# One stage for four of the five projections of the second block, 44 weight tiles through two slots, on one Trainium2 core

## The chip, the core and the metric

The kernel runs on one core of one Trainium2 chip. The metric is the device time of one execution in microseconds (us), the median of several executions of the same program. Below, PE is the matrix engine (TensorE), PEld its weight loads, ACT the scalar engine, DVE the vector engine, POOL the GpSimd engine and SP the engine that issues most of the DMAs (SPq is its queue).

## The reference

Two blocks run one after the other on x [1, 2048, 1024], all in float32. The first is a gated delta rule in both directions beside windowed attention. The change lies in the second, of which this is the part that matters:

```python
IN_SIZES = (D_ATT, D_ATT, D_ATT, D_ATT, D_CONV, D_CONV, D_CONV, D_CONV, D_MODEL, D_MODEL)  # 8 x 512, 2 x 1024
...
h = rmsnorm(x, norm_g[l])
proj = jnp.einsum('bsd,de->bse', h, w_in[l])                    # [2048, 1024] x [1024, 6144]
q, k, v, z_att, gb, gc, u, z_conv, g_att, g_conv = jnp.split(proj, IN_SPLITS, axis=-1)
att = chunked_rel_attention(q, k, v, rel_bias[l])
y_att = jnp.einsum('bsc,cd->bsd', att * jax.nn.silu(z_att), w_att_out[l])
vconv = causal_depthwise_conv(gc * u, conv_w[l], conv_b[l])     # 3 taps along the sequence
y_conv = jnp.einsum('bsc,cd->bsd', gb * vconv * jax.nn.silu(z_conv), w_conv_out[l])
m = jax.nn.sigmoid(g_att) * y_att + jax.nn.sigmoid(g_conv) * y_conv
x = x + jnp.einsum('bsd,de->bse', m, w_out[l])
```

## The kernel before

The program is a row of stages. Each stage is a `Ctx` (line 68): it takes its SBUF, PSUM and semaphores, runs a block with one instruction stream for each engine, waits for its last stores, and ends by clearing its semaphores and with a barrier over all engines (`__exit__`, line 78; the branches of line 79 in the rows stand for it). Nothing of a stage runs before the barrier of the one before it.

The stage group `dense2` in `build` (from line 2612) computes h and its products with `w_in_2`:

- `norm_transpose` ("n2", tiles named n_ in the profile) writes h transposed, as a rounded part `hi` and a remainder `lo`, [128, 8, 2048] each. Both stay in SBUF for the whole group.
- `project_features` "pq": queries and keys, 8 weight tiles, copied out.
- `project_rows` "pv": values, with the tokens on the partitions.
- `project_features` "pz": the gate z_att, 4 weight tiles, silu.
- `project_gated_conv` "gc": gc, u, gb and z_conv, 16 weight tiles, four for each of four groups of 128 channels.
- `project_features` "ps": the sigmoid gates, 16 weight tiles.

Chunk attention ("ca") follows. A weight tile is 1024 inputs by 128 outputs, [128, 8, 128], 512 KB. SP loads it into one of two slots (`wraw0`, `wraw1`), ACT rounds it (`whi`, lines 2100 and 2186), DVE makes the remainder (`wlo`, lines 2121 and 2214), and PE computes `feature_tile`: 4 column groups x 8 k x 3 products (hi*hi, hi*lo, lo*hi, lines 106 to 108) = 96 matmuls of 512 columns into a PSUM tile `pp0` or `pp1` of [128, 2048], four banks. The two slots alternate, so while PE works on one, the other is evicted and gets its next weights:

```python
for s in S:
    act.wait_ge(product[s], j + 1 + START)
    if more:
        split_hi(j + 1, s)
    act.wait_ge(stored[s], 16 * j + START)
    nc.scalar.activation(ob[s][:], pp[s][:], func).then_inc(copied[s], 1)
```

SP's queue in such a stage is, for each pair of tiles, two loads (each after the remainder of the tile before it in that slot exists) and then two stores (each after its eviction). In "gc" the order of a group is: gc is copied by ACT (line 2192), DVE multiplies it by u from PSUM (2227), runs three taps (2231, 2236), multiplies by gb from PSUM (2240) and, once ACT has made silu of z_conv (2202), by that (2246); SP then stores `acc` (2175). ACT, DVE and SP go through the first N - 1 steps in a hardware loop, PE through all of them, with 192 matmuls in a pass of its loop (384 in "gc"). `project_rows` (line 363) has its own loads, four pieces of 512 KB (line 399).

Of the kernel before, what the change touches and what calls it, by code (L numbers as in the profile page):

```python
# [30 lines left out]
ALU = mybir.AluOpType  # L31
# [3 lines left out]
P = 128  # L35
# [2097 lines left out]
def project_gated_conv(nc, w_tiles, conv_w, hi, lo, out):  # L2133

    PAD = 2
    with Ctx(nc, "gc") as c:
        raw, whi, wlo = weight_tiles(c)
        S = range(2)
        cw = c.sb("cw", [P, 4, 4])
        gcb = c.sb("gcb", [P, SEQ])  # L2140
        gu = c.sb("gu", [P, SEQ + PAD])
        acc = c.sb("acc", [P, SEQ])
        sz = c.sb("sz", [P, SEQ])
# [10 lines left out]
        gb_done = c.sem("gb_done")  # L2154
        z_done = c.sem("z_done")
        y_done = c.sem("y_done")
        stored = c.sem("stored")
        block = c.stack.enter_context(nc.Block())
        N = 4

        @block.sync
        def _(sp):
            sp.dma_start(cw[:], conv_w).then_inc(cw_in, 16)
            for s in S:
                sp.dma_start(raw[s][:], w_tiles[s]).then_inc(w_in[s], 16)

            def step(i, more):
                for q in range(4):
                    s = q % 2
                    if more or q < 2:  # L2170
                        sp.wait_ge(lo_ready[s], 2 * i + q // 2 + 1 + START)
                        sp.wait_ge(cw_in, 16 + START)
                        sp.dma_start(raw[s][:], w_tiles[4 * i + (2 + q)]).then_inc(w_in[s], 16)
                sp.wait_ge(y_done, i + 1 + START)
                sp.dma_start(out[i], acc[:]).then_inc(stored, 16)

            with sp.Fori(0, N - 1) as i:
                step(i, True)
            step(N - 1, False)
            sp.wait_ge(stored, 16 * N + START)  # L2180

        @block.scalar
        def _(act):
            def split_hi(n, s):
                act.wait_ge(w_in[s], 16 * n + 16 + START)
                nc.scalar.copy(whi[s][:], raw[s][:]).then_inc(hi_ready[s], 1)

            def step(i, more):
                act.wait_ge(product[0], 2 * i + 1 + START)
                split_hi(2 * i + 1, 0)  # L2190
                act.wait_ge(gu_done, i + START)
                nc.scalar.copy(gcb[:], pp[0][:]).then_inc(gc_copied, 1)
                act.wait_ge(product[1], 2 * i + 1 + START)
                split_hi(2 * i + 1, 1)
                act.wait_ge(product[0], 2 * i + 2 + START)
                if more:
                    split_hi(2 * i + 2, 0)
# [551 lines left out]
```

## Time and profile before

| what | value |
|---|---|
| median of 3 runs | 3802.14 us (3794.01 to 3803.87) |
| the profiled execution | 3789.2 us, span 3787.1 us |
| mean granted clock of PE | 0.923 of full |
| PE busy | 3256.6 us, 86% of the span |
| PE weight loads busy | 2696.8 us, 71% |
| DVE busy | 1307.0 us, 35% |
| ACT busy | 1081.6 us, 29% |
| POOL busy | 339.1 us, 9% |
| DMA | 382.43 MB, mean 101 GB/s |

The span is what the profiler saw of one execution; the device time of that execution is 2.1 us more, for what lies around it. Times within it are counted from the start of the span. The busy shares are means over stages with different limits, so the stretch from 1969 us (the first matmul of "pq") to 3101 us (the first of chunk attention) has to be read by itself. The ends of matmuls are modelled: a matmul of 512 columns is shown as 0.39 us while the next one starts earlier.

### The profile page before, as it was taken

How to read it: one execution, taken by the hardware profiler on the slowest of the kernel's cores; microseconds unless marked ns; L12 is line 12 of the kernel's file. 1: busy time of each engine (PE TensorE's matmuls, PEld its weight loads, DVE VectorE, ACT ScalarE, POOL GpSimd, SP SyncE). 2: the span in 40 equal slices, each digit the busy share in tenths (PEclk: the TensorE clock that was granted, in tenths of full speed). 3: DMA queues.
4: the chain of work that ended last, by engine and by line, in shares of the span. 5: the costliest groups of instructions: out<-in, count | busy, mean ns of one | idle time of the engine just before them, and what ended most of it. 6: DMA issues, size and time to landing. Idle time of an engine off the chain costs nothing. (4 is left out here: it accounts for less than half of the span.)

```text
span 3787.1 us, 60889 instructions
## 1 busy us (share of the span) xinstructions
PE 3256.6 (86%) x24054; PEld 2696.8 (71%) x24054; DVE 1307.0 (35%) x2392; ACT 1081.6 (29%) x2146; POOL 339.1 (9%) x316
## 2 busy tenths in 40 slices
PE   6996889754999973978959888999899979969899
PEld 5775779754999971546848777888688856747677
DVE  5554000263555547665540000111100015553343
ACT  4222111232444433871131111001022127740032
POOL 0000000001233224013200000000000001120000
PEclk8998999886999995998979999999999979989999
DMA  3122111384333334315531111010012133044453
GB/s 106 67 67 80 64 61 60 115 288 152 103 137 120 123 102 128 113 62 168 181 128 67 72 61 67 30 37 33 33 67 78 66 121 94 14 150 156 171 172 122
DMA packets 218819, 382.43 MB, mean 101 GB/s; under 512 B 34976, under 2 KB 143264, under 8 KB 202528
## 3 DMA queue, kind: packets, MB, share of 16 engines
q1 hardware_dynamic: 176512, 343.94, 26.6%
q10 hardware_dynamic: 42144, 36.18, 3.0%
q8 instruction: 119, 1.95, 0.2%
q14 instruction: 44, 0.36, 0.0%
HBM read 237.98 MB, written 142.08 MB: 100 GB/s over the span
## 5 line engine op out<-in xcount | busy, mean ns | idle before, releaser
L106 PE MATMUL ps_pp<-h_hi,ps_whi 128*128 128x512 f32 x512 | 200.1, 391 | 15.2 <-DVE ps_wlo L2121 15.2
L106 PE MATMUL gc_pp<-h_hi,gc_whi 128*128 128x512 f32 x512 | 200.2, 391 | 13.4 <-DVE gc_wlo L2214 13.4
L107 PE MATMUL ps_pp<-h_lo,ps_whi 128*128 128x512 f32 x512 | 199.9, 390 | 0.0
L107 PE MATMUL gc_pp<-h_lo,gc_whi 128*128 128x512 f32 x512 | 199.9, 390 | 0.0
L108 PE MATMUL gc_pp<-h_hi,gc_wlo 128*128 128x512 f32 x512 | 199.9, 390 | 0.0
L108 PE MATMUL ps_pp<-h_hi,ps_wlo 128*128 128x512 f32 x512 | 199.8, 390 | 0.0
L106 PE MATMUL pc_pp<-h_hi,pc_whi 128*128 128x512 f32 x384 | 152.8, 398 | 19.8 <-DVE pc_wlo L327 19.7
L107 PE MATMUL pc_pp<-h_lo,pc_whi 128*128 128x512 f32 x384 | 151.6, 395 | 0.0
L108 PE MATMUL pc_pp<-h_hi,pc_wlo 128*128 128x512 f32 x384 | 151.5, 395 | 0.0
L1626 POOL COPY ca_q<-ca_qr 128x512 f32 (+1 forms) x16 | 10.1, 632 | 1410.7 <-DMA ca_vr<-scratch_v_rows 1222.3
L1760 DVE CUSTOM_DVE_ANT_0 ca_neg<-ca_s,ca_bias 128x640 f32<-128x640 f32 (+4 forms) x128 | 92.0, 738 | 108.1 <-PE ca_s L1647 106.2
L2121 DVE TENSOR_TENSOR ps_wlo<-ps_wraw,ps_whi 128x1024 fp32r<-128x1024 f32 x16 | 19.6, 1225 | 300.4 <-ACT ps_whi L2100 300.4
L106 PEld LDWEIGHTS ps_pp<-h_hi,ps_whi 128*128 128x128 f32 x512 | 96.7, 189 | 35.8 <-issue 15.6
L106 PEld LDWEIGHTS gc_pp<-h_hi,gc_whi 128*128 128x128 f32 x512 | 96.7, 189 | 33.8 <-issue 13.8
L106 PE MATMUL fo_pp<-fo_whi,fo_mhi 128*128 128x512 f32 x256 | 100.9, 394 | 20.9 <-DVE fo_wlo L2541 20.9
L960 DVE COPY_PREDICATED ds_z<-ds_zmask,ds_ps 128x128 f32<-128x128 int32 x160 | 47.0, 300 | 196.1 <-PE ds_ps L1189 196.1
L338 DVE SCALAR_TENSOR_TENSOR pc_acc<-pc_pre,pc_taps,pc_acc 128x2048 f32<-128x2048 f32 x48 | 112.9, 2352 | 1.7
L1174 PE MATMUL ds_ps<-ds_ident,ds_u 64*64 64x64 f32 x2304 | 109.0, 226 | 2.7 <-issue 2.7
L107 PEld LDWEIGHTS gc_pp<-h_lo,gc_whi 128*128 128x128 f32 x512 | 96.7, 189 | 20.2
L1647 PE MATMUL ca_s<-ca_k,ca_q 64*128 64x512 f32 (+3 forms) x448 | 81.8, 478 | 33.9 <-DVE ca_k L1714 30.9
L107 PEld LDWEIGHTS ps_pp<-h_lo,ps_whi 128*128 128x128 f32 x512 | 96.6, 189 | 20.0
L108 PEld LDWEIGHTS gc_pp<-h_hi,gc_wlo 128*128 128x128 f32 x512 | 96.6, 189 | 20.0
(331 smaller groups left out, 7901.4 us busy)
## 6 DMA issues: line engine op xcount, KB each, us to landing
ds_pk<-scratch_pack SPq DMA_DIRECT2D x32, 1280.0 KB, 8.0
scratch_pack<-dp_out SPq DMA_DIRECT2D x16, 1024.0 KB, 4.2
scratch_sig_fm<-ps_ob SPq DMA_DIRECT2D x16, 1024.0 KB, 3.9
mb_sg<-scratch_sig_fm SPq DMA_DIRECT2D x16, 1024.0 KB, 6.9
scratch_qkv_fm<-pc_acc SPq DMA_DIRECT2D x12, 1024.0 KB, 4.8
dp_fm<-scratch_qkv_fm SPq DMA_DIRECT2D x16, 768.0 KB, 6.7
n_x<-in_x SPq DMA_DIRECT2D x16, 512.0 KB, 4.3
scratch_pack<-dp_out SPq DMA_DIRECT2D x16, 512.0 KB, 3.0
```

Of the source, the lines that this page charges most:

```text
L106: nc.tensor.matmul(out, ah, bh, start=(first and i == 0), stop=False)
L107: nc.tensor.matmul(out, ah, bl, start=False, stop=False)
L108: mm = nc.tensor.matmul(out, al, bh, start=False, stop=(last and i == n - 1))
L338: nc.vector.scalar_tensor_tensor(out=acc[s][:], in0=pre[s][:, t:t + SEQ], scalar=taps[s][:, t:t + 1], in1=acc[s][:], op0=ALU.mult, op1=ALU ...
L960: nc.vector.copy_predicated(z[d][:, n], zmask[:, d * NL + n, :].unsqueeze(1).to_broadcast([P, 4, QP]), ps[d][:, 0, 0:4 * QP].rearrange("p ...
L1174: return nc.tensor.matmul(ps[d][rows, 1, h * HP:(h + 1) * HP], source[rows, h, :], ident[rows, rows], start=True, stop=True)
L1626: nc.gpsimd.tensor_copy(q[s][:], qr[:, :, bass.ds(t * P, P)]).then_inc(qv_staged[s], 1)
L1647: mm = nc.tensor.matmul(s_ps[g][:, a:a + w], q[s][rows, m, :], k[s][rows, key_tile(m), a:a + w], start=True, stop=True)
L1760: nc.vector.tensor_tensor_reduce(neg[g][:, 0:n * P], s_ps[g][:, 0:n * P], bias_of(bias, h)[:, b0:b0 + n * P], -scale, sink[:, 1, h:h + 1] ...
L2121: nc.vector.tensor_tensor(wlo[s][:], raw[s][:], whi[s][:].bitcast(F32), ALU.subtract).then_inc(lo_ready[s], 1)
```

## The change

The first stage after the norm is now "pv". The other four projections become one stage "pj", `project_second`, over one array `w_second` of 44 weight tiles in the order of queries and keys (8), z (4), gated convolution (16), sigmoids (16); two tiles, one for each slot, are a step J, 22 steps in all (4, 2, 8, 8). Inputs, products and outputs stay as they were. The semaphores `copied`, `gc_copied`, `gu_done`, `gb_done` and `z_done` become one pair `freed`, counted through all of the stage; the conv's buffers `gcb` and `sz` become the two output buffers `ob0` and `ob1`. PE has one hardware loop of 22 passes; SP, ACT and DVE have straight code. Ahead of the convolution steps ACT waits for the stores of the last z tiles, and after them for the last product of the convolution (`y_done`), since those read or hold `ob0` and `ob1`. The four functions of the new stage are given in full, what they replace is printed above.

```diff
-def project_gated_conv(nc, w_tiles, conv_w, hi, lo, out):
+def project_second(nc, w_tiles, conv_w, hi, lo, qk, z, yconv, sig):
 
     PAD = 2
-    with Ctx(nc, "gc") as c:
+    J_QK, J_Z, J_GC, J_SIG = 4, 2, 8, 8
+    AT_Z = J_QK
+    AT_GC = AT_Z + J_Z
+    AT_SIG = AT_GC + J_GC
+    END = AT_SIG + J_SIG
+    with Ctx(nc, "pj") as c:
         raw, whi, wlo = weight_tiles(c)
         S = range(2)
+        ob = [c.sb(f"ob{s}", [P, SEQ]) for s in S]
...
-        gc_copied = c.sem("gc_copied")
-        gu_done = c.sem("gu_done")
+        freed = c.sems("freed", 2)
...
-        N = 4
+        features = ([(J, qk, 2 * J, J, ACT.Copy) for J in range(J_QK)] +
+                    [(J, z, 2 * (J - AT_Z), J, ACT.Silu) for J in range(AT_Z, AT_GC)])
+        sigmoids = [(J, sig, 2 * (J - AT_SIG), J - J_GC, ACT.Sigmoid) for J in range(AT_SIG, END)]
...
+        @block.sync
+        def _(sp):
+            def load_w(J, s):
+                if J > 0:
+                    sp.wait_ge(lo_ready[s], J + START)
+                sp.dma_start(raw[s][:], w_tiles[2 * J + s]).then_inc(w_in[s], 16)
+
+            def feature(J, out, n, k, func):
+                if J + 1 < END:
+                    for s in S:
+                        load_w(J + 1, s)
+                for s in S:
+                    sp.wait_ge(freed[s], J + 1 + START)
+                    sp.dma_start(out[n + s], ob[s][:]).then_inc(stored[s], 16)
+
+            for s in S:
+                load_w(0, s)
+            sp.dma_start(cw[:], conv_w).then_inc(cw_in, 16)
+            for job in features:
+                feature(*job)
+            for i in range(J_GC // 2):
+                J = AT_GC + 2 * i
+                for K in (J + 1, J + 2):
+                    for s in S:
+                        load_w(K, s)
+                sp.wait_ge(y_done, i + 1 + START)
+                sp.dma_start(yconv[i], acc[:]).then_inc(y_stored, 16)
+            for job in sigmoids:
+                feature(*job)
+            for s in S:
+                sp.wait_ge(stored[s], 16 * (END - J_GC) + START)
+            sp.wait_ge(y_stored, 16 * (J_GC // 2) + START)
+
+        @block.scalar
+        def _(act):
+            def split_hi(J, s):
+                act.wait_ge(w_in[s], 16 * J + 16 + START)
+                nc.scalar.copy(whi[s][:], raw[s][:]).then_inc(hi_ready[s], 1)
+
+            def feature(J, out, n, k, func):
+                for s in S:
+                    act.wait_ge(product[s], J + 1 + START)
+                    if J + 1 < END:
+                        split_hi(J + 1, s)
+                    act.wait_ge(stored[s], 16 * k + START)
+                    nc.scalar.activation(ob[s][:], pp[s][:], func).then_inc(freed[s], 1)
+
+            for s in S:
+                split_hi(0, s)
+            for job in features:
+                feature(*job)
+            for s in S:
+                act.wait_ge(stored[s], 16 * AT_GC + START)
+            for i in range(J_GC // 2):
+                J = AT_GC + 2 * i
+                act.wait_ge(product[0], J + 1 + START)
+                split_hi(J + 1, 0)
+                act.wait_ge(freed[1], J - 1 + START)
+                nc.scalar.copy(ob[0][:], pp[0][:]).then_inc(freed[0], 1)
+                act.wait_ge(product[1], J + 1 + START)
+                split_hi(J + 1, 1)
+                for s in S:
+                    act.wait_ge(product[s], J + 2 + START)
+                    split_hi(J + 2, s)
+                act.wait_ge(y_done, i + START)
+                nc.scalar.activation(ob[1][:], pp[1][:], ACT.Silu).then_inc(freed[1], 1)
+            act.wait_ge(y_done, J_GC // 2 + START)
+            for job in sigmoids:
+                feature(*job)
+
+        @block.vector
+        def _(dve):
+            def split_lo(J, s):
+                dve.wait_ge(hi_ready[s], J + 1 + START)
+                nc.vector.tensor_tensor(wlo[s][:], raw[s][:], whi[s][:].bitcast(F32),
+                                        ALU.subtract).then_inc(lo_ready[s], 1)
+
+            nc.vector.memset(gu[:, 0:PAD], 0.0).then_inc(edge, 1)
+            for s in S:
+                split_lo(0, s)
+            for J, *job in features:
+                for s in S:
+                    split_lo(J + 1, s)
+            dve.wait_ge(edge, 1 + START)
+            dve.wait_ge(cw_in, 16 + START)
+            for i in range(J_GC // 2):
+                J = AT_GC + 2 * i
+                split_lo(J + 1, 0)
+                dve.wait_ge(freed[0], J + 1 + START)
+                dve.wait_ge(product[1], J + 1 + START)
+                nc.vector.tensor_tensor(gu[:, PAD:PAD + SEQ], pp[1][:], ob[0][:], ALU.mult).then_inc(freed[1], 1)
+                split_lo(J + 1, 1)
+                dve.wait_ge(freed[1], J + 1 + START)
+                dve.wait_ge(y_stored, 16 * i + START)
+                nc.vector.tensor_scalar(acc[:], gu[:, 0:SEQ], cw[:, i, 0:1], cw[:, i, 3:4], ALU.mult,
+                                        ALU.add).then_inc(conv_done, 1)
+                for t in (1, 2):
+                    dve.wait_ge(conv_done, 3 * i + t + START)
+                    nc.vector.scalar_tensor_tensor(out=acc[:], in0=gu[:, t:t + SEQ], scalar=cw[:, i, t:t + 1],
+                                                   in1=acc[:], op0=ALU.mult, op1=ALU.add).then_inc(conv_done, 1)
+                dve.wait_ge(product[0], J + 2 + START)
+                dve.wait_ge(conv_done, 3 * i + 3 + START)
+                nc.vector.tensor_tensor(acc[:], pp[0][:], acc[:], ALU.mult).then_inc(freed[0], 1)
+                for s in S:
+                    split_lo(J + 2, s)
+                dve.wait_ge(freed[1], J + 2 + START)
+                dve.wait_ge(freed[0], J + 2 + START)
+                nc.vector.tensor_tensor(acc[:], ob[1][:], acc[:], ALU.mult).then_inc(y_done, 1)
+            for J, *job in sigmoids[:-1]:
+                for s in S:
+                    split_lo(J + 1, s)
+
+        @block.tensor
+        def _(pe):
+            with pe.Fori(0, END) as J:
+                for s in S:
+                    pe.wait_ge(lo_ready[s], J + 1 + START)
+                    pe.wait_ge(freed[s], J + START)
+                    feature_tile(nc, pp[s], whi[s], wlo[s], hi, lo).then_inc(product[s], 1)
...
     if stage("dense2"):
         with nc.sbuf_tensor("h2_hi", [P, KT, SEQ], F32R) as hi, nc.sbuf_tensor("h2_lo", [P, KT, SEQ], F32R) as lo:
             norm_transpose(nc, "n2", x1, d["norm_g"], d["consts"], hi, lo)
-            project_features(nc, "pq", d["w_qk2"], 8, hi, lo, qk_fm, ACT.Copy)
             project_rows(nc, "pv", d["w_v2"], 1, 512, hi, lo, v_rows)
-            project_features(nc, "pz", d["w_z2"], 4, hi, lo, z_fm, ACT.Silu)
-            project_gated_conv(nc, d["w_gc2"], d["conv2"], hi, lo, yconv_fm)
-            project_features(nc, "ps", d["w_sig2"], 16, hi, lo, sig_fm, ACT.Sigmoid)
+            project_second(nc, d["w_second"], d["conv2"], hi, lo, qk_fm, z_fm, yconv_fm, sig_fm)
     if stage("ca"):
         chunk_attention(nc, d, qk_fm, v_rows, att_fm)
     if stage("merge"):
@@ -2704,15 +2721,13 @@
         "w_out1": groups(np.concatenate([a["w_out"][0][:512], a["w_out"][0][512:].reshape(2, 4, HD, DM).transpose(
             1, 0, 2, 3).reshape(512, DM)], axis=0), DM)[0],
         "norm_g": a["norm_g_2"].reshape(1, DM),
-        "w_qk2": tiles_of(w2[:, 0:1024]),
         "w_v2": groups(w2[:, 1024:1536], 512),
-        "w_z2": tiles_of(w2[:, 1536:2048]),
-
-        "w_gc2": np.ascontiguousarray(tiles_of(w2[:, 2048:4096]).reshape(4, 4, P, KT, P)[[1, 2, 0, 3]].transpose(
-            1, 0, 2, 3, 4)).reshape(16, P, KT, P),
+        "w_second": np.concatenate([
+            tiles_of(w2[:, 0:1024]), tiles_of(w2[:, 1536:2048]),
+            tiles_of(w2[:, 2048:4096]).reshape(4, 4, P, KT, P)[[1, 2, 0, 3]].transpose(1, 0, 2, 3, 4).reshape(16, P, KT, P),
+            tiles_of(w2[:, 4096:])], axis=0),
         "conv2": np.ascontiguousarray(np.concatenate([a["conv_w_2"][0], a["conv_b_2"]], axis=0).reshape(
             4, 4, P).transpose(2, 1, 0)),
-        "w_sig2": tiles_of(w2[:, 4096:]),
         "rel_bias": rel_bias,
         "w_att2": tiles_of(a["w_att_out_2"][0]),
         "w_conv2": tiles_of(a["w_conv_out_2"][0]),
```

The first place is SP's queue where z ends and the convolution begins (wraw are the loads into the two slots, ob the stores of evicted tiles, L79 the barrier). Before:

```order
L2086 DMA scratch_z_fm<-pz_ob0 128x2048
L2086 DMA scratch_z_fm<-pz_ob1 128x2048
L79 UNCONDITIONAL_BRANCH
L2161 UNCONDITIONAL_BRANCH
L2163 DMA gc_cw<-in_conv2 128x16
L2165 DMA gc_wraw0<-in_w_gc2 128x1024
L2165 DMA gc_wraw1<-in_w_gc2 128x1024
```

The same place now:

```order
L2170 DMA pj_wraw0<-in_w_second 128x1024
L2170 DMA pj_wraw1<-in_w_second 128x1024
L2178 DMA scratch_z_fm<-pj_ob0 128x2048
L2178 DMA scratch_z_fm<-pj_ob1 128x2048
L2170 DMA pj_wraw0<-in_w_second 128x1024
L2170 DMA pj_wraw1<-in_w_second 128x1024
```

The two loads that used to follow the stores and a barrier (the first convolution tiles) now stand ahead of the last two stores of z, and the next two (the second pair of the convolution) right behind them.

The second place is ACT where the last group of the convolution ends and the sigmoids begin (CAST is the rounding of a weight tile, COPY and ACTIVATE evict PSUM). Before:

```order
L2186 CAST gc_whi0<-gc_wraw0 128x1024
L2192 COPY gc_gcb<-gc_pp0 128x2048
L2186 CAST gc_whi1<-gc_wraw1 128x1024
L2202 ACTIVATE gc_sz<-gc_pp1 128x2048
L79 UNCONDITIONAL_BRANCH
L2096 UNCONDITIONAL_BRANCH
L2100 CAST ps_whi0<-ps_wraw0 128x1024
L2100 CAST ps_whi1<-ps_wraw1 128x1024
```

The same place now:

```order
L2202 CAST pj_whi0<-pj_wraw0 128x1024
L2223 COPY pj_ob0<-pj_pp0 128x2048
L2202 CAST pj_whi1<-pj_wraw1 128x1024
L2202 CAST pj_whi0<-pj_wraw0 128x1024
L2202 CAST pj_whi1<-pj_wraw1 128x1024
L2230 ACTIVATE pj_ob1<-pj_pp1 128x2048
L2202 CAST pj_whi0<-pj_wraw0 128x1024
L2210 ACT_TABLE_LOAD
L2210 ACTIVATE pj_ob0<-pj_pp0 128x2048
```

The rounding of the first two sigmoid tiles now stands ahead of the last eviction of the convolution, as inside the convolution, and no barrier lies between.

## Rows read from the trace of the kernel before

**Rows 1.** The page: span, and busy time of each engine.
```profile
span 3787.1 us, 60889 instructions
PE 3256.6 (86%) x24054; PEld 2696.8 (71%) x24054; DVE 1307.0 (35%) x2392; ACT 1081.6 (29%) x2146; POOL 339.1 (9%) x316
```

**Rows 2.** Stretches: length, PE, PEld, DVE, ACT, POOL busy, PE clock, DMA share, GB/s.
```profile
2361.00:2711.00 350.00, 350.00 (x1536) 289.72 (x1536) 66.51 (x38) 27.17 (x21) 0.00 (x0) 0.99 0.09 30
2711.00:2726.60 15.60, 0.39 (x3) 0.02 (x1) 3.63 (x3) 3.97 (x3) 0.00 (x0) 0.58 0.36 134
2726.60:3077.00 350.40, 350.27 (x1536) 289.66 (x1536) 18.27 (x15) 60.33 (x44) 0.00 (x0) 0.99 0.18 66
```

**Rows 3.** Waits of PE, 1969 to 3080: us in total, times, longest.
```profile
PE ps_pp L106 <- DVE ps_wlo L2121: 15.2, 1, 15.2
PE gc_pp L106 <- DVE gc_wlo L2214: 13.4, 1, 13.4
PE pv_pp L106 <- DVE pv_wlo L426: 13.1, 1, 13.1
PE pz_pp L106 <- DVE pz_wlo L2121: 9.7, 1, 9.7
PE pq_pp L106 <- DVE pq_wlo L2121: 9.4, 1, 9.4
```

**Rows 4.** Timeline around the barrier between "gc" and "ps": start, length, engine, line.
```profile
2711.47 1.88 ACT L2202 ACTIVATE gc_sz<-gc_pp 128x2048 f32<-128x2048 f32 x1 [42.51 <-PE gc_pp L108]
2713.38 2.29 DVE L2246 TENSOR_TENSOR gc_acc<-gc_sz,gc_acc 128x2048 f32<-128x2048 f32 x1 [21.43 <-ACT gc_sz L2202]
2715.70 0.35 SPq L2175 DMA_DIRECT2D scratch_yconv_fm<-gc_acc  x1
2720.60 0.80 SPq L2089 DMA_DIRECT2D ps_wraw<-in_w_sig  x2
2724.15 1.04 ACT L2100 CAST ps_whi<-ps_wraw 128x1024 fp32r<-128x1024 f32 x1 [10.81 <-DMA ps_wraw<-in_w_sig]
2725.23 2.49 DVE L2121 TENSOR_TENSOR ps_wlo<-ps_wraw,ps_whi 128x1024 fp32r<-128x1024 f32 x2 [9.56 <-ACT ps_whi L2100]
```

**Rows 5.** First product's matmuls by tile: ns min/median/max, first and last start.
```profile
L106 PE MATMUL pq_pp<-h_hi,pq_whi x256: 389/389/790, 1969.0 to 2144.3; 128*128 128x512 f32 x128
L106 PE MATMUL pz_pp<-h_hi,pz_whi x128: 389/389/788, 2257.9 to 2346.7; 128*128 128x512 f32 x128
L106 PE MATMUL gc_pp<-h_hi,gc_whi x512: 389/389/790, 2360.9 to 2710.5; 128*128 128x512 f32 x171
L106 PE MATMUL ps_pp<-h_hi,ps_whi x512: 389/389/791, 2726.6 to 3076.0; 128*128 128x512 f32 x171
```

**Rows 6.** Stretches at and after the start of "ps", columns as in rows 2.
```profile
2726.50:2730.50 4.00, 3.91 (x9) 3.17 (x10) 1.22 (x1) 0.00 (x0) 0.00 (x0) 0.50 0.69 194
2730.50:3076.00 345.50, 345.50 (x1525) 286.13 (x1524) 17.15 (x14) 60.23 (x43) 0.00 (x0) 1.00 0.17 65
```

**Rows 7.** Timeline of PE, two matmuls in a row just after that start.
```profile
2728.03 0.63 PE L106 MATMUL ps_pp<-h_hi,ps_whi 128*128 128x512 f32 x1
2728.45 0.63 PE L107 MATMUL ps_pp<-h_lo,ps_whi 128*128 128x512 f32 x1
```

**Rows 8.** Timeline: first loads of "pq" and of "pv", first matmul of "pv".
```profile
1962.96 1.05 SPq L2089 DMA_DIRECT2D pq_wraw<-in_w_qk  x2
...
2152.01 2.11 SPq L399 DMA_DIRECT2D pv_wraw<-in_w_v  x4
...
2158.17 0.77 PE L106 MATMUL pv_pp<-pv_whi,h_hi 128*128 128x512 f32 x1 [13.07 <-DVE pv_wlo L426]
```

**Rows 9.** Timeline of ACT: an eviction inside "ps", with the wait ahead of it.
```profile
3055.15 1.88 ACT L2108 ACTIVATE ps_ob<-ps_pp 128x2048 f32<-128x2048 f32 x1 [18.93 <-PE ps_pp L108]
```

**Rows 10.** DMA issues: count, KB each, median us from issue to landing.
```profile
ps_wraw<-in_w_sig SPq DMA_DIRECT2D x16, 512.0 KB, 5.7
scratch_z_fm<-pz_ob SPq DMA_DIRECT2D x4, 1024.0 KB, 3.8
```

More of the change, by code:

```diff
@@ L2161, in _ @@
+        sigmoids = [(J, sig, 2 * (J - AT_SIG), J - J_GC, ACT.Sigmoid) for J in range(AT_SIG, END)]
         @block.sync
         def _(sp):
-            sp.dma_start(cw[:], conv_w).then_inc(cw_in, 16)
-            for s in S:
[L2165 to L2175, printed above, removed]
@@ L2182, in _ @@
+            for s in S:
+                sp.wait_ge(stored[s], 16 * (END - J_GC) + START)
+            sp.wait_ge(y_stored, 16 * (J_GC // 2) + START)
         @block.scalar
         def _(act):
-            def split_hi(n, s):
-                act.wait_ge(w_in[s], 16 * n + 16 + START)
+            def split_hi(J, s):
+                act.wait_ge(w_in[s], 16 * J + 16 + START)
                 nc.scalar.copy(whi[s][:], raw[s][:]).then_inc(hi_ready[s], 1)
[L2188 to L2197, printed above, removed]
-                act.wait_ge(product[1], 2 * i + 2 + START)
-                if more:
-                    split_hi(2 * i + 2, 1)
-                act.wait_ge(y_done, i + START)
-                nc.scalar.activation(sz[:], pp[1][:], ACT.Silu).then_inc(z_done, 1)
@@ L2235, in step @@
                     dve.wait_ge(conv_done, 3 * i + t + START)
-                    nc.vector.scalar_tensor_tensor(out=acc[:], in0=gu[:, t:t + SEQ], scalar=cw[:, bass.ds(i, 1), t],
+                    nc.vector.scalar_tensor_tensor(out=acc[:], in0=gu[:, t:t + SEQ], scalar=cw[:, i, t:t + 1],
                                                    in1=acc[:], op0=ALU.mult, op1=ALU.add).then_inc(conv_done, 1)
-                dve.wait_ge(product[0], 2 * i + 2 + START)
+                dve.wait_ge(product[0], J + 2 + START)
                 dve.wait_ge(conv_done, 3 * i + 3 + START)
-                nc.vector.tensor_tensor(acc[:], pp[0][:], acc[:], ALU.mult).then_inc(gb_done, 1)
-                if more:
-                    split_lo(2 * i + 2, 0)
-                    split_lo(2 * i + 2, 1)
-                dve.wait_ge(z_done, i + 1 + START)
-                dve.wait_ge(gb_done, i + 1 + START)
-                nc.vector.tensor_tensor(acc[:], sz[:], acc[:], ALU.mult).then_inc(y_done, 1)
-            with dve.Fori(0, N - 1) as i:
-                step(i, True)
-            step(N - 1, False)
+                nc.vector.tensor_tensor(acc[:], pp[0][:], acc[:], ALU.mult).then_inc(freed[0], 1)
[7 more added lines that the diff above has]
+                    split_lo(J + 1, s)
         @block.tensor
         def _(pe):
-            free = ((0, gc_copied, gb_done), (1, gu_done, z_done))
-            with pe.Fori(0, N) as i:
-                for q in range(4):
-                    s = q % 2
-                    pe.wait_ge(lo_ready[s], 2 * i + q // 2 + 1 + START)
-                    if q < 2:
-                        pe.wait_ge(free[s][2], i + START)
-                    else:
-                        pe.wait_ge(free[s][1], i + 1 + START)
+            with pe.Fori(0, END) as J:
+                for s in S:
+                    pe.wait_ge(lo_ready[s], J + 1 + START)
+                    pe.wait_ge(freed[s], J + START)
                     feature_tile(nc, pp[s], whi[s], wlo[s], hi, lo).then_inc(product[s], 1)
```

28 lines of the change are left out of this document (2 added, 26 removed).

## The prediction

> **What bounds the kernel now.** I read the page first: PE is busy for 86% of the span, the next engine for 35% [rows 1]. Such shares are means over all stages, so I asked for the stretches of the changed part. In them the picture is simple. While "gc" and "ps" run, PE is busy for 350.0 of 350.0 us and 350.3 of 350.4 us at a granted clock of 0.99, DVE for 67 us at most, ACT for 60, the DMA engines for 18%; in the 15.6 us between the two stages PE is busy for 0.4 us and its clock is 0.58 [rows 2]. So these stages are bound by the matmuls inside and by nothing but their ends between. The list of PE's waits says the same by name: from the first matmul of "pq" to the last of "ps" it holds five entries, one for each stage, each seen once, at its first matmul [rows 3]. There is no entry for a wait inside a stage.
>
> What such a gap is made of is best seen in the timeline at "gc" to "ps" [rows 4]: after the last matmul ACT evicts for 1.88 us, DVE multiplies for 2.29, SP issues the store at 2715.70; then 4.9 us pass (the store lands, semaphores are cleared, the barrier) until SP issues the first load of "ps" at 2720.60; 3.55 us later ACT starts to round it, DVE follows, and PE starts at 2726.6, which is 6.0 us after the load was issued.
>
> **What the change removes.** Before, PE starts five times in this part (pq, pv, pz, gc, ps). After, it starts twice (pv, pj). Each removed start has two terms.
>
> 1. *The wait.* The waits ahead of pv, gc and ps are 13.1, 13.4 and 15.2 us [rows 3]; together 41.7. The wait of 9.7 ahead of "pz" stays, as the one ahead of "pj": the same two loads and the same splits, after the same "pv". The wait ahead of the first stage stays too, but that stage is now "pv" in place of "pq". From its first load to its first matmul "pv" took 2158.17 - 2152.01 = 6.16 us and "pq" 1969.0 - 1962.96 = 6.04 [rows 5, 8], so 0.1 us is lost there. One correction: a wait is counted from the modelled end of the last matmul, 389 ns after its start [rows 5], while inside a stage the next matmul starts after 226 ns (next paragraph). That gives 0.16 us more for each removed wait, 0.5 in all.
>
> 2. *The slow first matmuls.* From the first to the last matmul of the first kind there are 349.6 us in "gc" (1533 steps) and 88.8 us in "pz" (381 steps) [rows 5]. The difference, 260.8 us over 1152 steps, gives 0.2264 us from start to start. Then 1533 steps are 347.1 us, and 2.5 us of "gc" are the price of starting; in the same way 2.3 for "ps" (349.4) and 2.1 for "pq" (175.3 less 765 steps, 173.2). The cause stands in the clock: in the first 4 us of "ps" the granted clock is 0.50, that is 1.2 GHz, and 9 matmuls run; behind them it is 1.00, 2.4 GHz [rows 6]. PE had been idle for 15.2 us before. At 0.50 two matmuls start 0.42 us apart [rows 7], 0.2 us more than at full clock, and nine of them make 1.8, the rest being the first matmul's own longer start. I take 2.3 us for each of three starts, 6.9.
>
> The Trainium skill (TensorE: Matmul & The Clock Gate, Part 1) gives 426.7 ns from start to start for 512 columns at the slow clock and 215.7 ns at the full one. An estimate with nine matmuls and that page's two figures is 1.9 us for a start, 5.7 for three, and a total of 47.8 in place of my 49.0. At full clock the trace disagrees with the page (226 ns, not 216), so the sum goes by the trace.
>
> Total: 41.7 + 0.5 - 0.1 + 6.9 = **49.0 us**.
>
> **What the change adds, and what covers it.** PE has the same 4224 matmuls in the merged stages, each at 0.2264 us, and one tile of 96 takes 21.7 us. That is the cover of everything else: when tile (J, 0) ends, PE works on (J, 1) for 21.7 us, and the weights of (J + 1, 0) need 1.04 us of ACT and 1.23 us of DVE (half of 2.49) [rows 4]. Inside "ps" ACT sat idle for 18.93 us ahead of an eviction, waiting for PE [rows 9]. Three places are new:
>
> - *z to convolution.* ACT now waits for the stores of the last z tiles before it may round the first tiles of the next step. The last store is issued after rounding and eviction (1.0 + 1.9 us behind the last z product) and lands in 3.8 us [rows 10]; the store of the other slot is 21.7 us older. So ACT is free some 7 us after that product, and the next product comes at 21.7. Nobody waits.
> - *convolution to sigmoids.* ACT waits for the last `y_done`: 1.0 (rounding) + 1.88 + 2.29 [rows 4], so 5.2 us behind the product, of 21.7. Behind it in SP's queue stand the store of `acc` and then the loads of the next sigmoid step. They go out near 5.6 us, land 5.7 us later at the median for such loads (this median holds the first loads of a stage, which have the DMA engines to themselves, and those beside stores) [rows 10], at about 11.3; ACT wants the first of them at 21.7. This is the tightest place, with 10 us to spare. If that cover were gone, PE would wait for the rest of the load and both splits.
> - *shared buffers and counts.* `ob0` and `ob1` in place of `gcb` and `sz`: within the convolution each is waited for at the points where gcb and sz were, so 0. The load of `cw` (8 KB) behind the first weights in place of ahead of them, one table load of ACT at each function change inside ACT's idle 18.9 us, and straight code on SP, ACT and DVE: 0, under the same cover. The last store of "pj" is that of "ps", so the passage to chunk attention stays as it is.
>
> For the straight code, the trace has no row of a fetch that stalls an engine. From below it costs nothing or even saves the branches, which are covered as well, so no gain; from above, only what exceeds about 18 us at one tile would reach PE. I take 0.
>
> **The sum.** The profiled execution took 3789.2 us (span 3787.1 and 2.1 around it); it would take 3789.2 - 49.0 = 3740.2. It lies 12.9 us (0.34%) below the median of the runs shown, and below the lowest of them, 3794.0. The gaps do not depend on what moves the runs, so the forecast goes from the median: 3802.1 - 49.0 = **3753.1 us**, a ratio of 0.987.
>
> **The rivals.**
>
> *A, the forecast* (0.86): three starts go in full. 3753.1. The known bounds of its terms are 41.7 (the clock gives nothing back) and 49.6 us (2.5 for each start), and the base may be any of the runs shown: 3794.0 - 49.6 = 3744.4 and 3803.9 - 41.7 = 3762.2.
>
> *B, a wait takes the place of a barrier* (0.06). At the two seams where the code differs (z to convolution, convolution to sigmoids) PE waits for weights, because SP holds the loads behind a store that waits for an eviction. For it: SP's queue is served in order, and both seams put a wait for DVE or ACT ahead of loads. Against it: the 10 us and more of slack above, and that "gc" has the same queue shape in each of its four groups without one wait of PE [rows 3]. Its price is at most the 6.0 us from load to first matmul at each seam [rows 4] and a slow start of 2.3: 2 x 8.3 = 16.6 us given back, 3769.7 us.
>
> *C, no change* (0.03): the gaps would have to be hidden by something else, or handed on, such as a longer start of chunk attention. Nothing in the trace works beside them; PE, ACT and DVE together are busy for 8 of 15.6 us there, one after the other [rows 2]. It would give 3802.
>
> *D, slower* (0.03): the clock. The longest dense stretch between 1969 us and chunk attention is 350 us, and its clock stays at 1.00 [rows 2, 6]; the new stage is 4224 x 0.2264 = 956 us without a pause, which nothing in this trace shows. If the granted clock fell to 0.50 somewhere behind the first 350 us, each matmul would cost 0.2 us more [rows 7]. The gain of 49.0 is used up after 245 matmuls at the low clock, about 105 us of it; with 302 of them the kernel is slower by 0.3%; and if all of the 606 us behind the first 350 (2677 matmuls) ran so, it would take 3753 + 535 = 4288 us. Against it: neither 350 us stretch shows a sign of a falling clock near its end. The same page of the Trainium skill knows a limiter that takes the clock to 13/16, but puts its start at the third core of a die under dense matmuls; by that rule one core stays at full clock, and the trace so far agrees.
>
> The last 0.02 is for a gain in the same direction of another size.
>
> **The numbers.** About 0.3%, 11.4 us, is what a measurement of this kernel can tell from no change. A, B and the rest are faster by more than that: 0.94. C is the same: 0.03. D is slower: 0.03. The range goes from 3738 (the best bound of A and 6 us of drift between executions) to 3770, which takes in A's worst bound and B's time; outside are C, D and tails of the others, under 2 in 10.
>
> **What the profile of the changed kernel would show.** PE's waits: one of about 9.7 us ahead of "pj", one near 9.5 ahead of "pv", no other up to chunk attention. First to last matmul of "pj" about 958 us (4224 x 0.2264 and 2.3), with a clock of 0.50 only in its first 4 us. From the first matmul of the part to the last of the first kind 3076.0 - 1969.0 = 1107.0 us [rows 5] become 1058. All other stages as before. The forecast is wrong if a second wait of PE stands inside "pj" (B), if the clock row there falls below 0.99 (D), or if the stretch behind the last product grows (C).

## The result, and the profile after

| | before | changed |
|---|---|---|
| median us (executions) | 3799.97 (4) | 3740.09 (4) |
| lowest to highest | 3794.01 to 3803.87 | 3732.47 to 3747.49 |
| span of the profiled execution | 3787.1 | 3730.7 |

The ratio is 0.9839, with a 95% interval of 0.9814 to 0.9864: a gain of 60 us where 49.0 were forecast, inside the forecast range of 3738 to 3770 but near its lower end. The ratios of this document leave out three executions, one each of e1_again, e2_four_stages and e4_stall (5618.56, 3969.16 and 10297.88 us), that were far slower than the others of the same kernel. There are two questions: are the 49 us there, and what are the other 11?

PE's waits in the changed kernel, from the end of the norm stage into chunk attention (us in total, times, longest), beside [rows 3]:

```profile
PE ca_s L1647 <- DVE ca_k L1714: 25.0, 1, 25.0
PE pv_pp L106 <- DVE pv_wlo L426: 11.2, 1, 11.2
PE pj_pp L106 <- DVE pj_wlo L2239: 9.6, 1, 9.6
```

Five waits of the projections have become two, and the one ahead of the merged stage is 9.6 us, as it was ahead of "pz" (9.7). No wait stands inside "pj". Its first kind of matmul, in the view by tile as in [rows 5], with the values' first:

```profile
L106 PE MATMUL pv_pp<-pv_whi,h_hi x128: 388/389/765, 1960.5 to 2049.8; 128*128 128x512 f32 x128
L106 PE MATMUL pj_pp<-h_hi,pj_whi x1408: 387/389/792, 2060.1 to 3019.5; 128*128 128x512 f32 x176
```

From the first projection matmul to the last of the first kind there were 3076.0 - 1969.0 = 1107.0 us [rows 5], and now 3019.5 - 1960.5 = 1059.0. That is 48.0 us less, where the sum said 49.0 and the last part of the prediction 1058. The stretches of the new stage, columns as in [rows 2]:

```profile
2060.00:2064.00 4.00, 3.85 (x9) 3.12 (x10) 1.24 (x2) 0.01 (x1) 0.00 (x0) 0.50 0.73 209
2064.00:2330.00 266.00, 266.00 (x1172) 220.30 (x1172) 14.71 (x12) 35.36 (x25) 0.00 (x0) 1.00 0.18 67
2340.00:2690.00 350.00, 350.00 (x1546) 290.00 (x1545) 70.22 (x40) 31.06 (x24) 0.00 (x0) 1.00 0.11 36
2690.00:3019.00 329.00, 329.00 (x1453) 272.61 (x1452) 17.16 (x14) 42.91 (x30) 0.00 (x0) 1.00 0.18 67
```

Nine matmuls at half the clock, then 1.00 to the end (the 10 us left out here as well): one slow start in place of four. In these 955 us of dense matmuls the clock does not fall; a fall was rival D.

The seam from the convolution to the sigmoids was named as the tightest place. ACT and SP there, from the timeline of the changed kernel (start, length, engine, line):

```profile
2672.19 1.05 ACT L2202 CAST pj_whi<-pj_wraw 128x1024 fp32r<-128x1024 f32 x1 [20.70 <-PE pj_pp L108]
2673.15 1.88 ACT L2230 ACTIVATE pj_ob<-pj_pp 128x2048 f32<-128x2048 f32 x1
...
2677.38 0.33 SPq L2191 DMA_DIRECT2D scratch_yconv_fm<-pj_acc  x1
2677.75 1.39 SPq L2170 DMA_DIRECT2D pj_wraw<-in_w_second  x2
...
2694.00 1.05 ACT L2202 CAST pj_whi<-pj_wraw 128x1024 fp32r<-128x1024 f32 x1 [18.97 <-PE pj_pp L108]
2695.07 1.28 ACT L2210 ACT_TABLE_LOAD   x1
```

ACT begins with the convolution's last product at 2672.2, SP's store goes out 5.2 us later and the loads at 5.6, as worked out; ACT uses the first of them 16.2 us after its issue, and then because PE had finished, not because of the load. The change of ACT's table, 1.28 us, fits in its idle time.

**Where the other 8 us of the profiled difference are.** They lie ahead of everything the change touches. These are the last remainders of the norm stage in the two kernels, DVE in the timeline. Before:

```profile
1957.31 4.61 DVE L223 TENSOR_TENSOR h_lo<-n_pt,h_hi 128x1024 fp32r<-128x1024 f32 x4
```

And in the changed kernel:

```profile
1948.15 4.61 DVE L223 TENSOR_TENSOR h_lo<-n_pt,h_hi 128x1024 fp32r<-128x1024 f32 x4
```

The norm stage ends at 1961.9 before and at 1952.8 now, 9.1 us earlier, with the same instructions in front of it. From there to the last projection matmul of the first kind it was 1114.1 us and is 1066.7, 47.4 less; behind it 711.1 and 711.2. 9.1 + 47.4 - 0.1 is the 56.4 us by which the spans differ. Whether the 9 us belong to the change (the weight arrays lie elsewhere in HBM, the program is shorter) or to the execution is what the first two experiments are for.

### The profile page after: what moved, and what is told of

The parts are those of the page before. It is cut to its first block and busy times, and to the rows that moved or that the text cites. A ratio compares the mean times of both kernels' runs of the same rounds, so it can differ in the third digit from the quotient of the medians.

```text
span 3730.7 us, 60457 instructions
## 1 busy us (share of the span) xinstructions
PE 3237.9 (87%) x24054; PEld 2683.2 (72%) x24054; DVE 1308.3 (35%) x2392; ACT 1061.7 (28%) x2132; POOL 337.4 (9%) x316
## 5 line engine op out<-in xcount | busy, mean ns | idle before, releaser
L106 PE MATMUL pj_pp<-h_hi,pj_whi 128*128 128x512 f32 x1408 | 549.3, 390 | 9.6 <-DVE pj_wlo L2239 9.6
L107 PE MATMUL pj_pp<-h_lo,pj_whi 128*128 128x512 f32 x1408 | 549.2, 390 | 0.0
L108 PE MATMUL pj_pp<-h_hi,pj_wlo 128*128 128x512 f32 x1408 | 549.1, 390 | 0.0
L106 PEld LDWEIGHTS pj_pp<-h_hi,pj_whi 128*128 128x128 f32 x1408 | 265.1, 188 | 64.7 <-issue 10.0
L108 PEld LDWEIGHTS pj_pp<-h_hi,pj_wlo 128*128 128x128 f32 x1408 | 265.0, 188 | 55.0
L107 PEld LDWEIGHTS pj_pp<-h_lo,pj_whi 128*128 128x128 f32 x1408 | 265.0, 188 | 55.0
L1189 PE MATMUL ds_ps<-ds_u,ds_neg_m 64*64 64x32 f32 x2560 | 102.7, 222 | 3.5 <-issue 3.5
L106 PE MATMUL mo_pp<-mo_whi,mo_mhi 128*128 128x512 f32 x256 | 103.2, 403 | 0.0
L108 PE MATMUL mo_pp<-mo_whi,mo_mlo 128*128 128x512 f32 x256 | 101.9, 398 | 0.0
L107 PE MATMUL mo_pp<-mo_wlo,mo_mhi 128*128 128x512 f32 x256 | 101.8, 398 | 0.0
```

The lines of the kernel that those rows point to most:

```text
L106: nc.tensor.matmul(out, ah, bh, start=(first and i == 0), stop=False)
L107: nc.tensor.matmul(out, ah, bl, start=False, stop=False)
L108: mm = nc.tensor.matmul(out, al, bh, start=False, stop=(last and i == n - 1))
L1189: mm = nc.tensor.matmul(ps[d][rows, 0, h * QP:(h + 1) * QP], neg_m[d][b][rows, h, rows], half(u[d][rows], LEVELS[n + 1], 1 - d)[:, h], sta ...
```

## The experiments

All ratios are to the kernel before, run on the same chip. The ratio of a whole run is uncertain by about 0.0025 (10 us), and by more from one comparison to the next: the changed kernel was measured three times, with 0.9839, 0.9868 and 0.9904, and the intervals of the first and the last do not touch. What is at stake is often less, so each profile is also read at three points: N, the end of the norm stage (where DVE's last remainder ends); A, from N to the first projection matmul; B, from there to the last projection matmul of the first kind. Every value is from a timeline or tile row like those above.

| kernel | N | A | B | ratio (interval) |
|---|---|---|---|---|
| before | 1961.9 | 7.1 | 1107.0 | 1 |
| changed | 1952.8 | 7.8 | 1059.0 | 0.9839 (0.9814 to 0.9864) |
| e1_again | 1962.5 | 8.0 | 1058.5 | 0.9868 (0.9844 to 0.9893) |
| e2_four_stages | 1966.6 | 7.6 | 1107.4 | 1.0004 (0.9986 to 1.0021) |
| e3_two_stages | 1974.8 | 7.9 | 1073.7 | 0.9913 (0.9890 to 0.9936) |
| e4_stall | 1955.8 | 7.9 | 1071.6 | 0.9933 (0.9910 to 0.9956) |
| e5_short_stall | 1975.8 | 7.6 | 1064.3 | 0.9885 (0.9862 to 0.9909) |
| e6_late_loads | 1977.5 | 7.8 | 1059.2 | 0.9877 (0.9852 to 0.9902) |
| e7_ahead | 1961.4 | 3.9 | 1053.2 | 0.9854 (0.9832 to 0.9876) |
| e8_pause_1us | 1953.2 | 7.9 | 1060.4 | one execution, 3737.9 us |
| e9_changed | 1958.8 | 7.8 | 1059.1 | 0.9904 (0.9881 to 0.9926) |
| e10_ahead | 1956.1 | 3.9 | 1053.5 | 0.9868 (0.9841 to 0.9896) |

**The same kernel again, and the merge alone undone.** The first has no edit. The second gives each projection a stage of its own by calling the new function four times:

```diff
-def project_second(nc, w_tiles, conv_w, hi, lo, qk, z, yconv, sig):
+def project_second(nc, name, steps, w_tiles, conv_w, hi, lo, qk, z, yconv, sig):
...
-    J_QK, J_Z, J_GC, J_SIG = 4, 2, 8, 8
+    J_QK, J_Z, J_GC, J_SIG = steps
...
-            project_second(nc, d["w_second"], d["conv2"], hi, lo, qk_fm, z_fm, yconv_fm, sig_fm)
+            project_second(nc, "p1", (4, 0, 0, 0), d["w_second"][0:8], d["conv2"], hi, lo, qk_fm, z_fm, yconv_fm, sig_fm)
+            project_second(nc, "p2", (0, 2, 0, 0), d["w_second"][8:12], ...)
+            project_second(nc, "p3", (0, 0, 8, 0), d["w_second"][12:28], ...)
+            project_second(nc, "p4", (0, 0, 0, 8), d["w_second"][28:44], ...)
```

> The changed kernel once more, for a second sample of its gain and of the stages ahead of the change. Theory R (the 9 us by which the stages before the first projection of the second block were shorter in the changed kernel's profile are chance between executions): its first matmul of 'pv' falls anywhere from 1958 to 1971 us, against 1960.5 and 1969.0 in the two profiles so far, while the stretch from there to the last matmul of 'pj' is again 1059 us. Theory L (the merged weight array or the shorter program lets the unchanged stages ahead run faster, every time): the first matmul of 'pv' is again at 1959 to 1962 us, and the ratio to before is 0.983 to 0.985, a gain of 58 to 65 us; R expects a gain nearer to 49 (ratio 0.987).

> The new code, the new order and the merged weight array, but with a stage of its own (with its barrier) for each of the four projections: the merge alone is undone. Theory A (the gain is the three removed starts): PE waits again about 13.4 us ahead of the second and third of them and 15.2 ahead of the fourth (queries to z has the same end and start as z to convolution), with a slow start of 2.3 each, so +49 us against the changed kernel and within 0.3% of the kernel before. Theory L (layout or straight code bring part of it): still 8 to 12 us faster than before.

In e2_four_stages guards at the ends of the loops, not printed above, leave out the loads and splits of a next step that its stage does not have. The changed kernel's second profile reaches N at 1962.5, later than the kernel before, and its ratio is 0.9868. With the merge undone but array, order and straight code kept, the ratio is 1.0004. The same view of that kernel:

```profile
1974.23 0.76 PE L106 MATMUL pv_pp<-pv_whi,h_hi 128*128 128x512 f32 x1 [9.93 <-DVE pv_wlo L426]
...
2073.49 0.79 PE L106 MATMUL p_pp<-h_hi,p_whi 128*128 128x512 f32 x1 [9.97 <-DVE p_wlo L2242]
...
2262.72 0.79 PE L106 MATMUL p_pp<-h_hi,p_whi 128*128 128x512 f32 x1 [13.01 <-DVE p_wlo L2242]
...
2365.64 0.79 PE L106 MATMUL p_pp<-h_hi,p_whi 128*128 128x512 f32 x1 [12.82 <-DVE p_wlo L2242]
...
2731.98 0.79 PE L106 MATMUL p_pp<-h_hi,p_whi 128*128 128x512 f32 x1 [15.38 <-DVE p_wlo L2242]
```

Three more waits, 13.0, 12.8 and 15.4 us, and B is back at 1107.4, which is 48.4 to 48.9 more than in the changed kernel's two profiles. So the gain in this stretch is the three removed starts, all of it; array, order and straight code bring nothing that shows. Theory L falls: in twelve profiles N lies anywhere from 1952.8 to 1977.5 us, over the same stages, and the changed kernel itself has it at 1952.8, 1962.5 and 1958.8. (e7_ahead and e10_ahead add one load to the norm stage; theirs lie inside that range.)

**One barrier put back**, by two calls, `(4, 2, 0, 0)` and `(0, 0, 8, 8)`.

> The changed kernel with one barrier put back, between z and the convolution: two stages of 12 and 32 weight tiles. Theory A: one wait of PE of 13.0 to 13.4 us (the cw load no longer comes ahead of the weights) and a slow start of 2.1 to 2.5 us, 15.3 to 16.1 us more than the changed kernel from the first matmul of 'pv' to the last of the sigmoids. If the clock gave nothing back, 13 us.

PE's waits in the two projection stages behind "pv":

```profile
PE p_pp L106 <- DVE p_wlo L2242: 22.9, 2, 13.0
```

The wait of 13.0 us is there, and B is 1073.7, 14.7 and 15.2 more than in the changed kernel's first two profiles. One start between z and the convolution thus costs about 15 us, just under the expected 15.3 to 16.1; less the wait and the 0.16 for the modelled end, 1.5 to 2.0 are left for the slow start.

**Pauses without a barrier.** Three kernels make PE wait at the same seam, ahead of the sigmoids, in one stage and with the weights ready. They differ in what it waits for:

```diff
-            with pe.Fori(0, END) as J:
-                for s in S:
-                    pe.wait_ge(lo_ready[s], J + 1 + START)
-                    pe.wait_ge(freed[s], J + START)
-                    feature_tile(nc, pp[s], whi[s], wlo[s], hi, lo).then_inc(product[s], 1)
+            with pe.Fori(0, AT_SIG) as J:
+                step(J)
+            pe.wait_ge(y_stored, 16 * (J_GC // 2) + START)     # e4_stall
+            pe.wait_ge(freed[1], AT_SIG + START)               # e5_short_stall
+            pe.wait_ge(hi_ready[1], AT_SIG + 1 + START)        # e8_pause_1us
+            with pe.Fori(AT_SIG, END) as J:
+                step(J)
```

(each kernel has one of the three waits; `step` is the removed loop body)

> The changed kernel, one stage, but PE waits ahead of the sigmoids until the last store of the convolution has landed; no barrier, no semaphore clearing, and the weights are ready by then. That is rival B made true at one seam. Expected idle time: 1.0 + 1.9 + 2.3 us to the last product of the convolution and about 4.5 for its store, 9.7 us. If the slow start hangs on the idle time alone, it comes back too (nine matmuls at a granted clock of 0.50, 2.1 to 2.5 us): +12 us in all. If it needs the barrier (a change of stage), the clock stays at 1.00 and the price is 9.7.

> As the kernel with the stall ahead of the sigmoids, but PE waits there only until ACT has evicted the last product of the convolution (about 1.0 + 1.9 us behind it), not for the product's way to HBM. Expected idle time 3 us. If the slow start follows any pause, nine matmuls at a clock of 0.50 come back (2.1 to 2.5 us, 5.3 in all); if it needs a pause of more than these 3 us (the shortest pause with a slow start seen so far is 9.5 us), the clock stays at 1.00 and the price is 3 us.

> As the short stall, but PE waits ahead of the sigmoids only until ACT has rounded the weights of the other slot, 1.05 us behind the last product of the convolution. The pause of 3.2 us had cost a slow stretch of nine matmuls that began 0.8 us after PE had resumed. If any pause is enough for that, nine matmuls at a clock of 0.50 appear again and the stretch from 'pv' to the last matmul of 'pj' is 1059 + 1.1 + 2 = 1062 us; if a pause of 1 us is ridden out, the clock stays at 1.00 and it is 1060 us.

The long stall, PE's timeline at the seam:

```profile
2685.94 0.79 PE L106 MATMUL pj_pp<-h_hi,pj_whi 128*128 128x512 f32 x1 [10.39 <-DMA scratch_yconv_fm<-pj_acc]
2686.53 0.63 PE L107 MATMUL pj_pp<-h_lo,pj_whi 128*128 128x512 f32 x1
```

PE idles for 10.4 us (9.7 had been expected), and from the second on the first matmuls take 0.63 us, at half the clock. B is 1071.6, which is 12.6 to 13.1 more: 10.4 of idle time, 0.16 for the modelled end, and 2.0 to 2.5 for the slow start. With 12 us expected if the slow start came back and 9.7 if it did not, the first is what came. So the slow start needs no barrier; it follows the pause. The short one:

```profile
2694.90 0.39 PE L108 MATMUL pj_pp<-h_hi,pj_wlo 128*128 128x512 f32 x1
2698.46 0.49 PE L106 MATMUL pj_pp<-h_hi,pj_whi 128*128 128x512 f32 x1 [3.17 <-ACT pj_ob L2230]
2698.79 0.40 PE L107 MATMUL pj_pp<-h_lo,pj_whi 128*128 128x512 f32 x1
2699.02 0.39 PE L108 MATMUL pj_pp<-h_hi,pj_wlo 128*128 128x512 f32 x1
2699.25 0.55 PE L106 MATMUL pj_pp<-h_hi,pj_whi 128*128 128x512 f32 x1
2699.60 0.63 PE L107 MATMUL pj_pp<-h_lo,pj_whi 128*128 128x512 f32 x1
...
2702.16 0.63 PE L107 MATMUL pj_pp<-h_lo,pj_whi 128*128 128x512 f32 x1
2702.59 0.47 PE L108 MATMUL pj_pp<-h_hi,pj_wlo 128*128 128x512 f32 x1
2702.89 0.39 PE L106 MATMUL pj_pp<-h_hi,pj_whi 128*128 128x512 f32 x1
```

A pause of 3.2 us is enough, against the second branch of what was expected. PE resumes at full clock, and only after the third matmul does the clock fall, while PE is busy again. B grows by 5.3 to 5.8 us for 3.2 us of waiting, so the slow stretch costs 2.0 to 2.5 us here too. With the third wait, PE's waits in the merged stage read:

```profile
PE pj_pp L106 <- DVE pj_wlo L2239: 9.9, 1, 9.9
PE pj_pp L106 <- ACT pj_whi L2202: 1.4, 1, 1.4
```

Here B is 1060.4, 1.4 and 1.9 more than the changed kernel's two first profiles: the pause itself, and no slow stretch. A pause of 1.4 us was ridden out and one of 3.2 us was not, each in a single profile; no limit follows from that, as the last section shows.

As whole runs, e4_stall came out dearer than its stretch: by the ratios of one comparison, 0.9933 beside 0.9868 for the changed kernel, it is 25 us slower, where the profile shows 13. With about 9 us of uncertainty on either side the excess is at the edge of what the runs can tell. Its profiled execution, 3748.1 us, was also the fastest of its seven and reached N early (1955.8). Whether the excess is drift or has a cause of its own stays open. e3_two_stages is 17 us above the changed kernel by its ratio and 15 by its stretch.

**The cover taken away.** Loads wait for the product, not for the remainder:

```diff
                 if J > 0:
-                    sp.wait_ge(lo_ready[s], J + START)
+                    sp.wait_ge(product[s], J + START)
                 sp.dma_start(raw[s][:], w_tiles[2 * J + s]).then_inc(w_in[s], 16)
```

> Every weight load of the merged stage is issued only when PE has finished the tile before it in its slot, not when that tile's remainder exists: up to 21 us later than now. This takes most of the cover that the prediction counted on. Theory A: behind the product come 3.6 us of load, 1.0 of ACT and 1.2 of DVE, about 6 us of the 21.7 that PE needs for the other slot, so PE waits nowhere in the stage and the stretch from the first matmul of 'pv' to the last of 'pj' stays at 1059 us. Rival B (the order of SP's queue decides): waits of PE appear at the steps where the loads stand behind stores, at least 2 to 6 us each, 10 us or more in all.

ACT's waits in this kernel over the projections, beside those of the changed one. With late loads:

```profile
ACT pj_whi L2202 <- DMA pj_wraw<-in_w_second: 823.2, 44, 28.5
```

In the changed kernel:

```profile
ACT pj_whi L2202 <- PE pj_pp L108: 812.1, 42, 24.7
ACT pj_whi L2202 <- DMA pj_wraw<-in_w_second: 6.7, 2, 6.5
```

Now every one of the 44 tiles is waited for by ACT, and PE still waits nowhere in the stage: B is 1059.2. The last tile shows what is left of the cover: its remainder is ready at 3008.3 us and its first matmul starts at 3023.4, 15 us later. The merged stage keeps its pace even with every load held back until its slot's product is done, so rival B was not near.

**A version with the two remaining starts shortened.** The norm stage loads the weights of "pv" at its end into a buffer that outlives it; "pv" loads, rounds and splits the first tile of the merged stage, which then starts with slot 0 ready (the remarks behind # name the place and are not in the kernel):

```diff
+            if ahead is not None:                                   # SP, norm_transpose, behind its last load of x
+                sp.dma_start(ahead[0], ahead[1]).then_inc(w_in, 16)
+                sp.wait_ge(w_in, 32 + START)
...
+            if tile_ahead is not None:                              # project_rows: SP, ACT, DVE
+                sp.dma_start(t_raw[:], t_src).then_inc(t_in, 16)
...
+                    act.wait_ge(t_in, 16 + START)
+                    nc.scalar.copy(t_hi[:], t_raw[:]).then_inc(t_hi_ready, 1)
...
+                    dve.wait_ge(t_hi_ready, 1 + START)
+                    nc.vector.tensor_tensor(t_lo[:], t_raw[:], t_hi[:].bitcast(F32), ALU.subtract)
...
+        nc.scalar.sem_inc(w_in[0], 16)                              # project_second, slot 0 of step 0 is there
+        nc.scalar.sem_inc(hi_ready[0], 1)
+        nc.scalar.sem_inc(lo_ready[0], 1)
```

> A version meant to beat both. The weights of 'pv' are loaded at the end of the norm stage, and the first weight tile of the merged stage is loaded and split while 'pv' runs. Of the 10 to 11 us of PE's wait ahead of 'pv' the load goes (3.6 us), of the 9.6 to 10 ahead of the merged stage load and splits go (6 us). Expected waits 7 and 4 us, 9.5 us less than the changed kernel, ratio to before 0.984. If the loads only collide with the last loads of the norm stage or delay its end, the first of the two gains is lost (6 us in all).

> The changed kernel beside the version with weights loaded ahead, on one chip. All local: the stretch from the end of the norm stage to the last matmul of 'pj' is 1067 us (7.8 to the first matmul of 'pv' and 1059), the ratio to before 0.985 to 0.988.

> The version with weights loaded ahead, once more, since its profile showed 9.7 us less between the end of the norm stage and the last matmul of 'pj' while its ratio (0.9854, with an interval of 0.0044) could not be told from the changed kernel's. Expected against the changed kernel of this comparison: 5 to 14 us less at the median; if it is equal or slower, the 9.7 us are given back elsewhere (a later stage, or a slower end of the norm stage).

PE's waits with the weights loaded ahead (the second of these profiles):

```profile
PE pv_pp L106 <- DVE pv_wlo L440: 6.2, 1, 6.2
PE pj_pp L106 <- ACTq L2181: 4.8, 1, 4.8
```

A is 3.9 us in both profiles in place of 7.8 to 8.0, B 1053.2 and 1053.5 in place of 1058.5 to 1059.1: together 9.1 to 9.8 us less than in the changed kernel's three profiles, where 9.5 had been expected. The waits are 6.9 and 6.2 us ahead of "pv" (7 expected) and 4.8 ahead of "pj" (4 expected). Side by side on one chip the medians are 3737.54 us and 3752.89, 15.4 us apart, somewhat more than the 5 to 14 expected. The changed kernel's stretch was as expected in e9_changed (7.8 + 1059.1 = 1066.9 us), its ratio was not (0.9904, expected 0.985 to 0.988); the ratios to before, 0.9868 (0.9841 to 0.9896) and 0.9904 (0.9881 to 0.9926), overlap at their ends, and e7_ahead's 0.9854 lies between the changed kernel's 0.9839 and 0.9868 of other comparisons. The gain in the stretch is shown; its size in the whole run is not measured better than some 10 us. It is the fastest of the versions by its two medians, 3736.17 and 3737.54.

## Why the prediction was right

- *The bound.* PE inside the stages, the ends between them: right. With the barriers back and all else kept, the time before is back (1.0004).
- *The waits.* 41.7 us for three. With the merge undone three waits came back with 13.0 + 12.8 + 15.4 = 41.2 us.
- *The slow first matmuls.* 2.3 us each, measured by itself in e4_stall at 2.0 to 2.5, in e3_two_stages at 1.5 to 2.0. The trace's figure held. The estimate by the Trainium skill (TensorE: Matmul & The Clock Gate, Part 1), 1.9 us, can't be told from it here. What the prediction left open is whether these 2 us hang on the pause or on the barrier: it is the pause.
- *The start of the first stage.* 0.1 us was set down for "pv" in place of "pq"; it was 0.7 (A is 7.8 against 7.1; 7.6 to 8.0 in the other profiles with the loads where they were). PE's wait ahead of "pv" came out at 11.2 us, where one near 9.5 had been forecast. Small, and the reading was thin: the load of "pv" was timed behind "pq", not behind the norm stage.
- *The merged stage.* 4224 x 0.2264 + 2.3 = 958 us; it took 959.4, since matmuls came 0.2267 us apart. With 0.6 from the line above and 1.5 from this one the sum of 49.0 would be 46.9; between N and the last matmul of the first kind the profiles show 47.4 (47.6 and 47.2 in the two later ones), against the one profile of the kernel before.
- *The cover.* The forecast of 5.2 and 5.6 us at the tightest seam was met to 0.1 us, and even late loads left PE busy.
- *The rivals.* B: no wait in the stage. C: the passage behind the last product is 711.2 us in place of 711.1. D: clock 1.00 over 955 us.
- *The total.* The mechanism and its price were right; that the first result lay in the range was partly luck. 3740.1 us is below the best bound of forecast A (3744.4) and stayed inside only by the 6 us of drift allowed for. The three comparisons gave 0.984, 0.987 and 0.990; their mean, 0.987, is the forecast, but with 25 us between the first and the last that agreement is chance too. Of the 56.4 us between the two profiled executions 9.1 lie in stages that the change doesn't touch. That the 11 us which the first comparison had in excess are the same drift is inferred from that and from the two later ratios; no profile was taken of the executions that make the medians. What was too small in the prediction is the base's drift: it allowed 6 us at the lower end, and N alone moves over a range of 24.7 us.

## What to carry to other kernels

Where an engine that is busy all through its stages stops only at their ends, the price of an end is read from one gap: last eviction, last store, barrier, first load, split, here 10 to 15 us, and about 2 us more for the matmuls that follow at half the clock. Merging stages takes it away whole if the next stage's weights have a slot, and then the cover of one tile (21.7 us) decides; if stages can't be merged, load and split the next one's first tile inside the one before (here 5 to 6 us off B, the stretch with "pj" in it). And before a surplus in a result is explained, look in the two traces at the point where the changed code begins.

## What the runs showed of the hardware

A pause of PE is paid after it as well. Granted clock around the short stall (stretches of 4 us, columns as in [rows 2]):

```profile
2694.00:2698.00 4.00, 1.29 (x6) 0.75 (x4) 1.22 (x1) 2.68 (x2) 0.00 (x0) 1.00 0.00 0
2698.00:2702.00 4.00, 3.54 (x10) 2.84 (x11) 2.29 (x1) 0.14 (x1) 0.00 (x0) 0.67 0.20 82
2702.00:2706.00 4.00, 4.00 (x17) 3.21 (x17) 0.00 (x0) 0.00 (x0) 0.00 (x0) 0.91 0.99 311
```

The clock was 1.00 while PE stood still and fell 0.8 us after it had started again. The expectation had asked whether a slow start would follow, not when. After the long stall the clock had fallen during the pause itself (0.50, DMA busy, PE not):

```profile
2682.00:2685.90 3.90, 0.00 (x0) 0.00 (x0) 0.00 (x0) 0.00 (x0) 0.00 (x0) 0.50 0.97 296
```

The same effect makes part of the drift ahead of N. In the first block's convolution stage ("pc") PE waits about 10 us at the start and then pauses five times, for 1.7 to 2.1 us, at the same places of the same code. In the changed kernel's first profile no slow stretch follows any of the five:

```profile
60.00:335.00 275.00, 265.74 (x1150) 216.58 (x1149) 130.16 (x66) 63.50 (x42) 0.00 (x0) 0.99 0.18 61
153.50:157.50 4.00, 3.75 (x16) 3.11 (x17) 3.43 (x3) 0.63 (x1) 0.00 (x0) 1.00 0.00 0
```

With one barrier put back, a change that lies some 2000 us later, one follows each of them:

```profile
60.00:335.00 275.00, 264.72 (x1122) 216.57 (x1122) 131.01 (x66) 64.23 (x42) 0.00 (x0) 0.96 0.17 57
154.00:158.00 4.00, 3.75 (x10) 2.93 (x11) 3.42 (x3) 0.63 (x1) 0.00 (x0) 0.57 0.00 0
```

(The second row of each pair is the second of the five pauses.) The twelve profiles hold 60 such pauses. Behind the 27 of 1.69 to 1.76 us no slow stretch came; behind the 33 of 2.03 to 2.09 us it came 22 times and cost about 1.6 us each time. In 21 of the 22 the first matmul behind the pause was still at full clock, as in e5_short_stall. So a pause of 2 us can go either way in the same code, and the single profiles of e5_short_stall and e8_pause_1us draw no line between 1.4 and 3.2 us. The 9.5 us that the expectation of e5_short_stall named as the shortest pause with a slow start was not the shortest on hand: "pc" has them at 2.0 us in the profile of the kernel before. Nor is it shown that length alone decides, for every pause of 1.7 us stands behind one that had no slow stretch.

From its first to its last matmul "pc" took 276.0 us in the changed kernel's first profile and 282.2 in that of e3_two_stages, 6.1 of the 22.0 us by which N differs between them. What moves the rest was not looked into and stays open, but whole executions point the same way: over the 17 of the kernel before beside e1_again the mean granted clock goes from 0.925 down to 0.918 and the time from 3780.7 up to 3805.1 us, in the main longer where the clock is lower.
